# Hybrid encoder step on one core: V sums on TensorE as four 64x64 pieces, x1 rows added in the same way, score matmuls of two components alternating

## What is computed

```python
s = einsum('bqhcd,bkhcd->bhcqk', q, k) * (HEAD_DIM ** -0.5)   # two components c of 64 channels per head
a = softmax(s)[:, :, 0] - lam * softmax(s)[:, :, 1]           # differential attention, then a @ v
...
x  = x + mix @ w_o                                            # called x1 in the kernel
s_top, i_top = top_k(s, 16)                                   # product keys, 8 heads, 16 experts each
h  = gelu(einsum('nkd,nd->nk', u[e], xt))                     # 128 expert rows of U per row of x
f  = einsum('nk,nkd->nd', g * h, v[e])                        # 128 expert rows of V per row of x
x  = x + f
```

## Time and profile before

| | |
|---|---|
| median of three runs | 4329.8 us |
| the profiled execution's own time | 4324.57 us |
| its span, first to last instruction | 4322.8 us |
| mean granted clock of TensorE | 0.938 of full speed |
| TensorE matmul busy | 3606.8 us (83%) |
| VectorE busy | 2726.5 us (63%) |
| ScalarE busy | 1506.1 us (35%) |
| GpSimd busy | 1540.1 us (36%) |
| moved by DMA | 1363.85 MB, mean 316 GB/s |
| V sums, TensorE, L998 | 3208 matmul records, 1616 us busy |
| diagonals, ScalarE, L1223 | 802 |

### The profile page before, as it was taken

How to read it: one execution, slowest core, us unless ns; L and a number is a source line. 1 busy time by engine, 2 the same in 40 slices (tenths; PEclk the granted TensorE clock), 3 DMA queues, 4 the chain that set the end, 5 groups by cost and what they waited for, 6 DMA issues and landing times.

```text
span 4322.8 us, 39516 instructions
## 1 busy us (share of the span) xinstructions
PE 3606.8 (83%) x10764; PEld 1876.9 (43%) x10764; DVE 2726.5 (63%) x6194; ACT 1506.1 (35%) x4350; POOL 1540.1 (36%) x1424
## 2 busy tenths in 40 slices
PE   5777998778888999998889887996788877777777
PEld 3444555434444555454344443564535422222222
DVE  3333200277887779655877878775877576576774
ACT  2111101135555234332445545223433333333332
POOL 1111000044544334323544454433444443444443
PEclk8888999889999999998999998998899999999999
DMA  5222333388978999998978898999999999999998
GB/s 180 70 70 70 102 101 120 102 343 315 352 290 333 356 411 416 348 371 344 371 293 331 324 345 325 390 385 348 416 390 408 366 419 420 418 411 420 409 398 339
DMA packets 264701, 1363.85 MB, mean 316 GB/s; under 512 B 32224, under 2 KB 71904, under 8 KB 129056
## 3 DMA queue, kind: packets, MB, share of 16 engines
q0 software_dynamic: 154656, 1116.80, 65.1%
q1 hardware_dynamic: 80720, 210.05, 13.5%
q10 hardware_dynamic: 29104, 34.48, 2.2%
HBM read 1321.50 MB, written 39.73 MB: 315 GB/s over the span
## 4 chain that ended last, share of the span: by engine, by line
PE 48%; DMA 20%; DVE 15%; issue 6%; ACT 5%; DVEq 2%; POOL 1%; SPq 1%; ACTq 1%; POOLq 0%
PE tl_ps L998 15%; DMA mix<-in_peer_uv,tl_idx 9%; PE tl_ps L947 8%; DMA ringx<-in_peer_uv,tl_idx 8%; PE tl_ps L790 7%; PE tl_ps L983 4%; PE tl_ps L931 4%; PE tl_ps L959 3%; DVE mix L1579 3%; PE tl_ps L849 2%; DVE ringx L1579 2%; PE tl_ps L772 2%; DVE tl_mx L1384 1%; DVE tl_xa L1590 1%; DMA low<-in_watt 1%
## 5 line engine op out<-in xcount | busy, mean ns | idle before, releaser
L998 PE MATMUL tl_ps<-mix,tl_dg 128*128 128x512 f32 x1840 | 926.8, 632 | 223.1 <-ACT tl_dg L1223 207.7
L730 POOL DMA_INDIRECT mix<-in_peer_uv,tl_idx x604 | 721.3, 1194 | 1082.1 <-PE tl_ps L998 715.9
L1579 DVE CUSTOM_DVE_ANT_0 mix<-mix,tl_xb 128x1024 f32<-128x1024 f32 x604 | 735.4, 1222 | 368.0 <-DMA mix<-in_peer_uv,tl_idx 352.9
L730 POOL DMA_INDIRECT ringx<-in_peer_uv,tl_idx x452 | 547.6, 1212 | 783.7 <-PE tl_ps L998 540.6
L998 PE MATMUL tl_ps<-ringx,tl_dg 128*128 128x512 f32 x1368 | 689.5, 633 | 126.8 <-ACT tl_dg L1223 121.0
L1212 ACT ACTIVATE tl_hg<-tl_hd 128x1 f32<-128x1 f32 x1056 | 213.0, 202 | 1427.8 <-DVE tl_hd L1579 1411.4
L1579 DVE CUSTOM_DVE_ANT_0 ringx<-ringx,tl_xb 128x1024 f32<-128x1024 f32 x452 | 550.6, 1223 | 239.9 <-DMA ringx<-in_peer_uv,tl_idx 229.2
L998 PEld LDWEIGHTS tl_ps<-mix,tl_dg 128*128 128x128 f32 x1840 | 340.0, 198 | 674.5 <-ACT tl_dg L1223 376.8
L998 PEld LDWEIGHTS tl_ps<-ringx,tl_dg 128*128 128x128 f32 x1368 | 255.8, 199 | 473.6 <-ACT tl_dg L1223 243.7
L947 PE MATMUL tl_ps<-tl_xr,low 128*128 128x384 f32 (+1 forms) x1280 | 386.9, 459 | 29.2 <-DMA low<-in_wall 28.3
L1223 ACT ACTIVATE tl_dg<-ident,tl_hw 128x128 f32<-128x128 f32 x802 | 322.0, 401 | 68.2 <-PE tl_ps L998 10.5
(11 more groups left out here) (175 smaller groups left out, 3903.3 us busy)
## 6 DMA issues: line engine op xcount, KB each, us to landing
low<-in_wall SPq DMA_DIRECT2D x240, 512.0 KB, 3.6
low<-in_watt SPq DMA_DIRECT2D x72, 512.0 KB, 4.5
mix<-in_peer_uv,tl_idx POOLq DMA_INDIRECT x604
sc_rows<-tl_stage ACTq DMA_DIRECT2D x36, 256.0 KB
tl_sch<-sc_rows POOLq DMA_DIRECT2D x18, 512.0 KB
ringx<-in_peer_uv,tl_idx POOLq DMA_INDIRECT x452
xn_t<-mix SPq DMA_DIRECT2D x1, 4224.0 KB, 12.1
n_xt<-in_x_prompt SPq DMA_DIRECT2D x8, 512.0 KB, 7.1
```

Source lines behind the costliest of these rows:

```text
L730: nc.gpsimd.indirect_dma_start(out=ring[q % RING].rearrange("p a d -> p (a d)"), out_offset=None, in_=A["peer_uv"], in_offset=bass.Indirec ...
L998: last = nc.tensor.matmul(acc[:, h * 512:(h + 1) * 512], dg[:, npe(q) % DIAGS, :], ring[q % RING][:, 1, h * 512:(h + 1) * 512], start=k == ...
L1579: nc.vector.tensor_tensor_reduce(out=ring[q % RING][:, 0, :], in0=ring[q % RING][:, 0, :], in1=xb[:, t % 2, :], scale=1.0, scalar=0.0, op0 ...
```

## The change

V sums: the diagonal matrix is stored as two 64x64 diagonals above each other (`dg` is 128x64, made from `eye`, two stacked 64x64 identities), and a slot's V sum becomes four matmuls. Matmul (b, h) takes rows 64b to 64b+63 and columns 512h to 512h+511 of the V rows and writes 64 partitions: half h of bank b. Each uses its own fourth of the array. `acc` so holds row r of half b and column c of half h at partition 64h + r, column 512b + c. The x1 rows with VectorE's sums are added on TensorE too, by four matmuls with pieces of `ident` (`add_start`), at the end of a tile; ScalarE copies `acc` to `xa` at k = 0 of the next tile (VectorE's `add_part` is gone), issues the store at once, as two DMAs, and reloads `xa` at k = 6. VectorE may now take slots from k = 14 on. DIAGS goes from 4 to 8. The score matmuls of a call alternate between the components, piece by piece.

```diff
--- before.py
+++ after.py
@@ -36,7 +36,7 @@
 RING = 7
 WRING = 6
 QUAD = 4
-DIAGS = 4
+DIAGS = 8
 
 
 BLOCKS = ((0, 3 * P, (0, 1, 2)), (3 * P, 3 * P, (3, 4, 5)), (6 * P, 2 * P + DEC, (6, 7, 8)))
@@ -258,7 +258,7 @@
 def by_dve(q):
 
     t, k = divmod(q, SLOTS)
-    if not (4 if t == 0 else 30) <= k < SLOTS - 4:
+    if not (4 if t == 0 else 14) <= k < SLOTS - 4:
         return False
     return any(first <= q < end and q * share % whole < share for first, end, share, whole in SHARED)
 
@@ -315,6 +315,11 @@
     return sum(turns(BLOCKS[x // 24][2][x % 3]) for x in range(w))
 
 
+def half_of(b):
+
+    return slice(b * P // 2, (b + 1) * P // 2)
+
+
 def stored_keys(g):
 
     return 16 * (g // 2 + 1) if g < 16 else 16 * 8 + 32 * (g // 2 - 7)
...
@@ -425,9 +430,11 @@
         hd = sb("hd", [P, TOPK])
         hg = sb("hg", [P, TOPK])
         hw = sb("hw", [P, TOPK])
-        dg = sb("dg", [P, DIAGS, P])
+        dg = sb("dg", [P, DIAGS, P // 2])
+        eye = sb("eye", [P, P // 2])
         ps = ctx.enter_context(nc.psum_tensor("tl_ps", [P, 8, 512], F32))
         acc = ps[:, 0:2, :].rearrange("p a b -> p (a b)")
+        quarters = [(b, h) for h in range(2) for b in range(2)]
         ident, ut = keep["ident"], keep["ut"]
         block = ctx.enter_context(nc.Block())
 
@@ -650,7 +657,7 @@
             for par in range(2):
                 sp.wait_ge(s[f"k_out{par}"], stored_keys(3 * DC - 1))
                 sp.wait_ge(s[f"v_out{par}"], stored_keys(3 * DC - 1))
-            sp.wait_ge(s["y_out"], 16 * (NT + 1))
+            sp.wait_ge(s["y_out"], 32 * NT + 16)
 
         @block.gpsimd
         def _(pool):
@@ -658,6 +665,7 @@
             nc.gpsimd.memset(ssx[:], 1.0)
             nc.gpsimd.memset(qss[:], 1.0)
             nc.gpsimd.memset(sel[:], 0.0)
+            nc.gpsimd.memset(eye[:], 0.0)
             nc.gpsimd.iota(iou[:], pattern=[[1, TOPK]], base=0, channel_multiplier=0)
             pool.drain()
             nc.gpsimd.tensor_copy(iot[:], iou[:])
@@ -666,6 +674,10 @@
             for q in range(4):
                 nc.gpsimd.affine_select(out=sel[:], in_=sel[:], compare_op=ALU.not_equal, fill=1.0, base=-DEC * q,
                                         pattern=[[-1, DEC]], channel_multiplier=1)
+                pool.drain()
+            for q in range(2):
+                nc.gpsimd.affine_select(out=eye[:], in_=eye[:], compare_op=ALU.not_equal, fill=1.0, base=-(P // 2) * q,
+                                        pattern=[[-1, P // 2]], channel_multiplier=1)
                 pool.drain()
             pool.sem_inc(s["sel_done"], 1)
 
@@ -756,22 +768,25 @@
                 def score(g, i, components):
                     t, w = tiles[i], 3 * g + i
                     n, par = rows_of(t), g % 2
-                    for c in components:
-                        pe.wait_ge(s["tq_c"], 3 * g + i + 1)
-                        if rb and i == 0 and c == 0:
+                    pe.wait_ge(s["tq_c"], 3 * g + i + 1)
+                    if components[0] == 0:
+                        if rb and i == 0:
                             pe.wait_ge(s[f"kp_in{par}"], 16 * ((g - DC) // 2 + 1))
-                        if t == NT and c == 0:
+                        if t == NT:
                             pe.wait_ge(s["kc_in"], 16 * (g - 2 * DC + 1))
-                        if w:
-                            pe.wait_ge(s["ex_d"], 2 * w + c if t == NT else 2 * w)
-                        if w >= 2 and c == 0:
+                        if w >= 2:
                             pe.wait_ge(s["ot_c"], w - 1)
-                        rows = slice(c * HD, (c + 1) * HD)
-                        o = scores(t, n, c)
-                        for k, keys in keys_of_unit(rb, par, rows, i, t):
-                            last = nc.tensor.matmul(o[:, k:k + keys.shape[1]], qTh[rows, par, i * P:i * P + n], keys,
+                    if w:
+                        pe.wait_ge(s["ex_d"], 2 * w + components[0])
+                    rows = [slice(c * HD, (c + 1) * HD) for c in range(2)]
+                    keys = [keys_of_unit(rb, par, rows[c], i, t) for c in range(2)]
+                    for j, (k, _) in enumerate(keys[0]):
+                        for c in components:
+                            src = keys[c][j][1]
+                            last = nc.tensor.matmul(scores(t, n, c)[:, k:k + src.shape[1]], qTh[rows[c], par, i * P:i * P + n], src,
                                                     start=True, stop=True)
-                        last.then_inc(s["sc_d"], 1)
+                            if j + 1 == len(keys[0]):
+                                last.then_inc(s["sc_d"], 1)
 
                 def project(g, i):
                     t, j = tiles[i], 3 * g + i
@@ -993,12 +1008,22 @@
                 pe.wait_ge(s["dg_done"], npe(q) + 1)
                 if k == 0 and t:
                     pe.wait_ge(s["part_done"], t)
-                final = SLOTS - 1 if t < NT else DEC - 1
-                for h in range(2):
-                    last = nc.tensor.matmul(acc[:, h * 512:(h + 1) * 512], dg[:, npe(q) % DIAGS, :],
-                                            ring[q % RING][:, 1, h * 512:(h + 1) * 512], start=k == 0,
-                                            stop=k == final, skip_group_check=True)
+                for b, h in quarters:
+                    rows = half_of(b)
+                    last = nc.tensor.matmul(ps[half_of(h), b, :], dg[rows, npe(q) % DIAGS, :],
+                                            ring[q % RING][rows, 1, h * 512:(h + 1) * 512], start=k == 0,
+                                            stop=t == NT and k == DEC - 1, skip_group_check=True)
                 last.then_inc(s["used_pe"], 1)
+
+            def add_start(t):
+                pe.wait_ge(s["xa_in"], 16 * (t + 1))
+                if ndve((t + 1) * SLOTS):
+                    pe.wait_ge(s["used_dve"], ndve((t + 1) * SLOTS))
+                for b, h in quarters:
+                    rows = half_of(b)
+                    last = nc.tensor.matmul(ps[half_of(h), b, :], ident[rows, rows], xa[rows, h * 512:(h + 1) * 512],
+                                            start=False, stop=True, skip_group_check=True)
+                last.then_inc(s["summed"], 1)
 
             steps = [started(part(rb)) for rb in range(PASSES) for part in (attend, middle)]
             first = 0
@@ -1008,11 +1033,15 @@
                 for at in range(first, q - LAG + 1 if q + 1 < LAST else LAST):
                     if not by_dve(at):
                         weigh(at)
+                    if at % SLOTS == SLOTS - 1:
+                        add_start(at // SLOTS)
                 first = max(q - LAG + 1, 0)
             pe.wait_ge(s["sel_done"], 1)
             pe.wait_ge(s["acc_done"], NT + 1)
-            for h in range(2):
-                last = nc.tensor.matmul(ps[:DEC, 2 + h, :], sel[:], xb[:, 1, h * 512:(h + 1) * 512], start=True, stop=True)
+            for b in range(2):
+                for h in range(2):
+                    last = nc.tensor.matmul(ps[:DEC, 2 + h, :], sel[half_of(h), :], xb[half_of(h), 1, b * 512:(b + 1) * 512],
+                                            start=b == 0, stop=b == 1)
             last.then_inc(s["fin_d"], 1)
 
         @block.scalar
@@ -1220,7 +1249,7 @@
                     act.drain()
                     if npe(q) >= DIAGS:
                         act.wait_ge(s["used_pe"], npe(q) - DIAGS + 1)
-                    nc.scalar.activation(dg[:, npe(q) % DIAGS, :], ident[:], ACT.Copy, scale=hw[:, j:j + 1]).then_inc(s["dg_done"], 1)
+                    nc.scalar.activation(dg[:, npe(q) % DIAGS, :], eye[:], ACT.Copy, scale=hw[:, j:j + 1]).then_inc(s["dg_done"], 1)
 
             def load_x1(t):
 
@@ -1243,6 +1272,7 @@
                 for step in steps:
                     advance(step, q)
                 if q == -6:
+                    act.wait_ge(s["sel_done"], 1)
                     load_row(0)
                     load_x1(0)
                 if q < 0:
@@ -1251,11 +1281,16 @@
                     slot(q - ACT_LAG)
                 if k == 64 and t < NT:
                     load_row(t + 1)
-                if k == 8 and t:
+                if k == 0 and t:
+                    act.wait_ge(s["summed"], t)
+                    nc.scalar.copy(xa[:], acc).then_inc(s["part_done"], 1)
+                    act.drain().then_inc(s["acc_done"], 1)
                     act.wait_ge(s["acc_done"], t)
-                    act.dma_start(A["y_prompt"][0, (t - 1) * P:t * P, :], xa[:]).then_inc(s["y_out"], 16)
-                if k == 20 and t:
-                    act.wait_ge(s["y_out"], 16 * t)
+                    for h in range(2):
+                        act.dma_start(A["y_prompt"][0, (t - 1) * P:t * P, h * 512:(h + 1) * 512].rearrange("(b r) c -> r b c", b=2),
+                                      xa[half_of(h), :].rearrange("p (b c) -> p b c", b=2)).then_inc(s["y_out"], 16)
+                if k == 6 and t:
```

(12 more changed lines are left out.)

2 lines of the change are left out of this document (1 added, 1 removed).

## The result

The changed kernel takes 4258.9 us (median of 4 runs, 4251.39 to 4260.71) against 4330.87 us: a ratio of 0.9831, with a 95% interval from 0.9813 to 0.9848. That is 72 us less, where 90 were predicted. The profiled execution took 4257.62 us (span 4255.8), 67 us less than the one before.

A forecast was written before the change was run, and what follows sets the result against it. After 865 us a chain through several engines was taken as the bound, DMA alone in the tail. Two thirds of 108 + 21 = 129 us, plus 11 for the tail, less 8, gave 89 us: 4235.6 profiled, 4240 us predicted, range 4130 to 4370.

The forecast's parts named there:

- scores alternate: Attention stretches: alternating the components' score matmuls saves a third of their chain time, 4 + 17 = 21 us.
- tile end: Eight tile ends: final sums on TensorE and ScalarE's copy cost about 1 us more each, 8 us.
- 47 rows to VectorE: Slots from k = 14: 60 us more on VectorE, 59 us less on TensorE; counted zero, 30 us either way.
- V sums packed: Four mixed stretches: a slot costs 1.25 instead of 1.72 us; capped by DMA room, 24 + 22 + 39 + 23 = 108 us.
- tail filled up: Last stretch, DMA bound at 2.49 us a slot: only dips in the rate can fill, up to 11 us.
- The mechanism: Each V sum slot: four quarters side by side, both passes each, 0.86 us; mixed slots some 1.25 us with switch and load.
- The rival with pairs: V sums: column halves don't overlap, slot keeps 1.72 us and pays switches; about 4420 us, chance 0.15.
- I count two thirds: Mixed stretches: of 129 us off the chain, 86 us counted, since other steps run close beside it.
- The room for DMA: After 865 us: about 217 us can be won before DMA alone is the bound, 22 of them in the first middle.
- my cap: Last middle stretch: 39 us of V sum saving limited to 23 us of DMA room, at share 0.97.
- The clock rival: Three mixed stretches: clock falls 0.06, 60 us on the chain plus 30 for VectorE's rows; 4315 to 4335 us, chance 0.14.
- one of the signs that I had named against the forecast: Mixed stretches: the forecast would be wrong if the granted clock fell below 0.9.

The follow-up runs named there:

- 0.9862: Changed kernel with VectorE's V rows again only from k = 30 on, so 47 rows go back to TensorE: 4267.5 us, 0.9862 of the kernel before.
- 0.9824: The changed kernel itself measured again, as base of its group: 4247.71 us, 0.9824 of the kernel before.
- 0.9976: The kernel before with only the alternating score order added: 4314.17 us, 0.9976 of the kernel before.
- 0.9999: Changed kernel with V sums, x1 rows and final sums in old form, four diagonal buffers, VectorE's rows from k = 30: 4327.81 us, 0.9999 of the kernel before.
- 0.9934: Changed kernel with V sums, x1 rows and final sums in old form, four diagonal buffers, VectorE's rows from k = 14: 4295.3 us, 0.9934 of the kernel before.
- the other two runs: Profiled runs with packed V sums: the changed kernel again, 4247.71 us, and the changed kernel with four diagonal buffers in place of eight, 4251.84 us.
- the one with filler: Changed kernel with four 64x64 zero matmuls of 256 columns ahead of V sums of slots 1 to 727, except at k = 0: 4279.83 us, 0.9893.

## Why the prediction was right

The time lies in the range and 19 us above the point. That it came so near is in part luck: V sums and tail brought 24 + 11 us less than counted, and the rows, counted as zero, brought 28. Without the 47 rows 60 us would have been won (0.9862), not 76 (0.9824). With the ratios of the runs (times 4326 us) the change comes apart in a chain of one part after the other:

| part | counted | measured | by |
|---|---|---|---|
| scores alternate | -14 (21, two thirds) | -10 | 0.9976 |
| tile end | +8 | +10 | 0.9999 against 0.9976 |
| 47 rows to VectorE | 0 (up to 30 to either side) | -28; -16 with packed sums | 0.9934 against 0.9999; 0.9862 against 0.9824 |
| V sums packed | -72 (108, two thirds) | -48; -59 without the 47 rows | 0.9824 against 0.9934; 0.9862 against 0.9999 |
| tail filled up | -11 | 0 | GB/s of the tail |

The parts in the order scores, tile end, rows, V sums add up to the whole by construction. Where a part has two values, it depends on what else is in place.

**The mechanism** was right in each step of a slot: all four quarters at once, both passes of each, a switch of 0.10 us, 1.22 us in place of 1.25. Starts were to show four passes and the next four 0.43 us later; they came 0.48 us later. The rival with pairs is out: its slot would have been 1.72 us.

**The size of the V sum term** is where the forecast missed: the measured value is 18 to 33% below the 72 us counted, and the step that failed is the deduction "I count two thirds", taken from all stretches alike. Between 44% (48 of 108) and 55% of the capped term came. The traces show where: 352 us of V sums left the chain, and steps of VectorE and gathers took their place. In attention of block 1 the same slots took 6 us less (in the other two runs 9 and 13), though 24 us had been found there and 4 for the scores, and VectorE's rows and dots stood in the chain; taking the rows off it in both attention stretches gave 26 to 30 us. The room for DMA was rightly seen as the bound in the first middle, where the share reached 1.00 and the rate 403 GB/s: 22 us of room were counted, and 29 us came with all that changed there. In the last middle my cap was too wide: I had taken its share of 0.97 for 23 us of room, and 6 came. Every kernel with packed V sums but the one with filler needs 741 to 746 us for these slots, whatever VectorE's rows, and the full V sums with the 47 rows 747. What keeps the share at 0.97 there was not tried.

**VectorE's rows** were counted as zero, and are a gain of 16 to 28 us. TensorE was so much scarcer in the first middle stretch than VectorE, at 97% against 72% busy, that time of the two should not have been set against each other one to one: the 22 us that I gave to packing there were won by the rows already (share 0.99 with full V sums too). Slots 145 to 296 took 544 us before, 542 with full V sums and rows from k = 30, 521 with rows from k = 14, 528 with packed V sums and rows from k = 30, and 515 in the changed kernel, which has both.

**The tail** won nothing; its rate was 414 GB/s before and after. The dips in the rate did not go away with the shorter V sum; where they come from was not tried.

**The clock rival** was half right: the clock did fall below 0.9 in three mixed stretches, one of the signs that I had named against the forecast. It fell by 0.06 to 0.09 there, as much as the rival had asked for, and 72 us came all the same; VectorE's rows, a loss of 30 us in the rival's sum, were a gain. The dense matmuls of the middle stretches and of the projection are busy for longer, as the profile page of the changed kernel shows (their means before were 459, 527, 480 and 447 ns):

```profile
L962 PE MATMUL tl_ps<-tl_xr,low 128*128 128x384 f32 (+1 forms) x1280 | 402.1, 472 | 31.1 <-DMA low<-in_wall 29.4
L805 PE MATMUL tl_ps<-low,tl_xr 128*128 128x384 f32 (+1 forms) x768 | 332.9, 588 | 32.2 <-ACT tl_u L1104 18.3
L998 PE MATMUL tl_ps<-tl_xr,low 128*128 128x384 f32 (+1 forms) x768 | 260.4, 493 | 6.2 <-ACTq L1196 6.2
L946 PE MATMUL tl_ps<-tl_xr,low 128*128 128x384 f32 (+1 forms) x768 | 237.0, 465 | 0.6 <-ACT tl_xr L1083 0.6
```

By the difference of the means times the counts that is 17 + 47 + 10 + 14 = 88 us of busy time. How much of it lies on the chain was not measured, and how many of the missing 19 us it explains stays open; filler that raised the clock cost more than it brought. In the last middle it seems to cost nothing: 744 us at 0.93 without rows on VectorE, 745 at 0.86.

The rule of the Trainium skill ("TensorE: Matmul & The Clock Gate", Part 3) that matmuls start strictly in program order doesn't hold pass by pass here: four passes start within 0.02 us, so first passes of later quarters start before the second passes of earlier ones, which come 0.48 us after the first. For whole matmuls of two passes this trace doesn't contradict it. The measured packing of four row tiles in the same part of the Trainium skill, 3.07 times, compares with 3.44 / 1.02 = 3.4 times for this slot, counted from its start to the start of the next dense matmul.

## What to carry to other kernels

A float32 matmul with a diagonal or otherwise block-wise stationary operand can be cut into 64x64 pieces, each with its own fourth of the array, and takes 0.6 of the time (1.02 against 1.72 us), or 0.7 where it stands between matmuls on the whole array. Once an operation has become that much cheaper on one engine, the division of work between engines that was tuned for its old price has to be set anew, stretch by stretch: this gave 26 to 30 us on top of 72. A shorter operation on the chain gives back only what the next engine's chain and the DMA room leave, so both are to be read for each stretch before its share is counted; here 352 us left the chain for 48 to 59 us of time. A DMA share a few per cent under full need not be room: the stretch at 0.97 stayed at 0.97. Compare two kernels by the same work and not by the same times.
